# Handing a span's row lists on head by head: where the first expert fetches of a span stand in its search

## The reference, cut to what matters

```python
def peer_block(h, w_peer_q, sub_keys, expert_u, expert_v):
    q = (h @ w_peer_q).reshape(t, PEER_HEADS, 2, PEER_HALF)
    s = jnp.einsum('thcd,chnd->thcn', q, sub_keys, preferred_element_type=jnp.float32)
    s1, i1 = lax.top_k(s[:, :, 0], PEER_TOPK)
    s2, i2 = lax.top_k(s[:, :, 1], PEER_TOPK)
    cand = (s1[..., :, None] + s2[..., None, :]).reshape(...)
    best, sel = lax.top_k(cand, PEER_TOPK)
    eidx = jnp.take_along_axis(cidx, sel, axis=-1)
    g = jax.nn.softmax(best, axis=-1).astype(h.dtype)
    a = jax.nn.gelu(jnp.einsum('thkd,td->thk', expert_u[eidx], h), approximate=False)
    return jnp.einsum('thk,thkd->td', g * a, expert_v[eidx])
```

## Time and profile before

| What | us |
| --- | --- |
| median of 3 runs | 3914.27 |
| the profiled execution, its own time | 3925.3 |
| its span in the profile | 3923.5 |
| VectorE busy | 2617.0 (67%) |
| TensorE busy | 3260.3 (83%) |
| GpSimd busy | 1120.7 (29%) |

### The profile page before, as it was taken

How to read it: one execution, slowest core, us unless ns; L and a number is a source line. 1 busy time by engine, 2 the same in 40 slices (tenths; PEclk the granted TensorE clock), 3 DMA queues, 4 the chain that set the end, 5 groups by cost and what they waited for, 6 DMA issues and landing times.

```text
span 3923.5 us, 36349 instructions
## 1 busy us (share of the span) xinstructions
PE 3260.3 (83%) x10704; PEld 1824.9 (47%) x10704; DVE 2617.0 (67%) x5677; ACT 1405.3 (36%) x4207; POOL 1120.7 (29%) x1252
## 2 busy tenths in 40 slices
PE   6797898488999987777888899877788887787887
PEld 4423787245555443344544454423444444575431
DVE  1364117777757996777687779964777676756874
ACT  1122201485123233666522233333454444222343
POOL 0000001333323333333333334342333333323442
PEclk9897799788999999888899999998888988676899
DMA  2112243699999989999999999998898888999999
GB/s 92 33 36 67 91 150 102 259 399 404 397 364 408 363 316 372 411 407 406 376 426 426 426 414 378 377 389 344 325 368 350 338 360 336 391 401 412 425 421 385
DMA packets 234020, 1289.23 MB, mean 329 GB/s; under 512 B 45468, under 2 KB 59868, under 8 KB 98341
## 3 DMA queue, kind: packets, MB, share of 16 engines
q0 software_dynamic: 152064, 1107.36, 69.5%
q1 hardware_dynamic: 80036, 175.22, 12.6%
q10 hardware_dynamic: 1728, 4.39, 0.3%
HBM read 1273.47 MB, written 13.40 MB: 328 GB/s over the span
## 4 chain that ended last, share of the span: by engine, by line
PE 35%; DMA 27%; DVE 16%; ACT 5%; issue 5%; POOL 1%; SPq 1%; ACTq 0%; DVEq 0%; POOLq 0%
DMA tl_uv<-in_uv,tl_idx 23%; PE tl_y L905 12%; PE tl_f L1151 6%; DVE tl_uv L1490 3%; PE tl_f L1131 3%; PE tl_f L1162 3%; DVE tl_acc L1477 2%; PE tl_f L1177 2%; DMA X<-in_krope 2%; PE tl_f L965 1%; PE tl_f L1075 1%; PE tl_f L1098 1%; DVE tl_eq L1574 1%; POOL tl_uv L837 1%; PE tl_f L1017 1%
## 5 line engine op out<-in xcount | busy, mean ns | idle before, releaser
L1490 DVE CUSTOM_DVE_ANT_0 tl_uv<-tl_uv,tl_h 128x1024 f32<-128x1024 f32 x1056 | 1272.4, 1217 | 706.4 <-DMA tl_uv<-in_uv,tl_idx 680.4
L837 POOL DMA_INDIRECT tl_uv<-in_uv,tl_idx x1056 | 1042.4, 987 | 1941.1 <-PE tl_y L905 1378.7
L905 PE MATMUL tl_y<-tl_uv,tl_diag 128*128 128x512 f32 (+1 forms) x2552 | 1318.6, 659 | 254.9 <-ACT tl_diag L1198 254.8
L905 PEld LDWEIGHTS tl_y<-tl_uv,tl_diag 128*128 128x128 f32 (+1 forms) x2552 | 491.0, 204 | 916.5 <-issue 497.9
L1226 ACT ACTIVATE tl_ge<-tl_a 128x1 f32<-128x1 f32 x1056 | 209.0, 198 | 1248.1 <-DVE tl_a L1490 1246.5
L1477 DVE SCALAR_TENSOR_TENSOR tl_acc<-tl_uv,tl_w,tl_acc 128x1024 f32<-128x1024 f32 x410 | 524.9, 1280 | 67.2 <-ACT tl_w L1210 66.5
L1210 ACT ACTIVATE tl_w<-tl_ge,tl_weight 128x1 f32<-128x1 f32 x1024 | 301.5, 294 | 33.2
L849 POOL TENSOR_TENSOR tl_cand<-tl_tv 128x48 f32<-128x48 f32 (+5 forms) x128 | 66.1, 544 | 784.2 <-DVE tl_ti L1522 626.1
L1151 PE MATMUL tl_f<-H,w_tail 128*128 128x384 f32 (+2 forms) x1024 | 266.0, 417 | 11.6 <-DMA w_tail<-in_w_merge 7.7
L1177 PE MATMUL tl_f<-H,w_tail 128*128 128x384 f32 (+2 forms) x1024 | 265.8, 414 | 10.2 <-DVE H L1717 9.6
L1198 ACT ACTIVATE tl_diag<-K,tl_w 128x128 f32<-128x128 f32 (+1 forms) x638 | 253.6, 397 | 34.4 <-PE tl_y L905 14.1
(11 more groups left out here) (213 smaller groups left out, 3119.4 us busy)
## 6 DMA issues: line engine op xcount, KB each, us to landing
w_tail<-in_w_merge SPq DMA_DIRECT2D x96, 512.0 KB, 7.6
w_tail<-in_w_peer SPq DMA_DIRECT2D x64, 576.0 KB, 7.7
w_tail<-in_w_conv SPq DMA_DIRECT2D x48, 512.0 KB, 7.9
tl_uv<-in_uv,tl_idx POOLq DMA_INDIRECT x1056, 11.4
w_tail<-in_w_mix SPq DMA_DIRECT2D x32, 512.0 KB, 7.6
X<-in_cache SPq DMA_DIRECT2D x64, 128.0 KB
X<-in_x SPq DMA_DIRECT2D x8, 536.0 KB, 6.9
o_y<-tl_acc ACTq DMA_DIRECT2D x8, 512.0 KB, 6.3
```

What stands on the lines that cost most here:

```text
L837: pool.indirect_dma_start(UV[:, u % RING, :], None, d["uv"], bass.IndirectOffsetOnAxis(ap=which, axis=0)).then_inc(landed[u % RING], 16)
L905: mm = pe.matmul(Y[0:m, half * 512:(half + 1) * 512], DG[:, (pe_count[u] - 1) % DIAGS, 0:m], UV[:, u % RING, D + half * 512:D + (half + 1) ...
L1490: dve.tensor_tensor_reduce(UV[:, u % RING, 0:D], UV[:, u % RING, 0:D], HP[:], 1.0, 0.0, ALU.mult, ALU.add, A[:, t % 2, i:i + 1]).then_inc( ...
```

## The change

Heads are put into groups, `HEADS`: in spans 0 to 2 the groups end after head 1, 2, 4 and 8 (of 8), in span 3 there is one. ScalarE's exponential (`powers`) and VectorE's three operations (`shares`) run once for each group, two search steps after the group's last list, and `gset` counts groups. GpSimd no longer waits for `ranked` before a span's first unit but, in the first tile of a span, for the `finish` of the head whose picks it is to fetch. `due` opens the units of a span's own first tile inside its search: `EDGE` says how far the units are at each span's end (56, 296, 696, 1024 in place of 0, 256, 640, 1024), and the units from one edge to the next are spread over the whole of a span (25/25; 23/25 in the last). In span 0's search TensorE does 4 units a step from step 7 on. `by_dve` follows the new places: 450 units are VectorE's, against 418.

```diff
+        HEADS = [[1, 2, 4, PH]] * (NCH - 1) + [[PH]]
+        group = lambda c, h: next(k for k, e in enumerate(HEADS[c]) if h < e)
+        groups_to = lambda c, k: sum(len(x) for x in HEADS[:c]) + k
+        weighed_at = lambda h: 2 * h + 5
+        EDGE = [56, begin[1] + 40, begin[2] + 56, begin[3]]
...
         def due(c, i, lag):
             if c == 0:
-                return 0
-            first, last = begin[c - 1], begin[c]
-            at = passed[c][i + PRE[c]]
-            base = first + (last - first) * 23 * at // (25 * passed[c][-1])
-            return min(base + lag, last, last if lag == LAG_POOL else -(-(base + (base % PICK == 0)) // PICK) * PICK)
+                base = 4 * max(0, i - RANK - 6)
+            else:
+                at = passed[c][i + PRE[c]] * (23 if c == NCH - 1 else 25)
+                base = EDGE[c - 1] + (EDGE[c] - EDGE[c - 1]) * at // (25 * passed[c][-1])
+            open_to = begin[c]
+            if c < NCH - 1:
+                open_to += TOPK * max([e for e in HEADS[c] if i - RANK >= (weighed_at(e - 1) + 2 if e < PH else HC + 4)], default=0)
+            return min(base + lag, open_to, open_to if lag == LAG_POOL else -(-(base + (base % PICK == 0)) // PICK) * PICK)
...
             def issue(u):
-                if u == begin[c]:
+                if t == PARTS[c][0] and t < NP - 1 and i % TOPK == 0:
+                    pool.wait_ge(finished, 2 * (c * PH + i // TOPK + 1))
+                if t == NP - 1 and i == 0:
                     pool.wait_ge(ranked, c + 1)
-                if t == NP - 1 and i == 0:
                     pool.wait_ge(spread, 4)
...
                 for q in range(HC):
+                    if c == 0 and q == 5:
+                        turn(0)
                     units(due(c, RANK + q, 0))
...
-                if c == 0:
-                    turn(0)
...
-                if u == begin[c]:
-                    act.wait_ge(gset, c + 1)
+                if t == PARTS[c][0] and (i == 0 or t < NP - 1 and i % TOPK == 0 and i // TOPK in HEADS[c]):
+                    act.wait_ge(gset, groups_to(c, (group(c, i // TOPK) if t < NP - 1 else 0) + 1))
...
+                def powers(k):
+                    first, past_ = ([0] + HEADS[c])[k:k + 2]
+                    act.wait_ge(paired, (c * PH + past_) * PAIR)
+                    w = GW[:, c % 2, 0:nt, first * TOPK:past_ * TOPK]
+                    act.activation(w, w, ACT.Exp).then_inc(expo, 1)
...
+            def shares(c, k, nt):
+                first, past_ = ([0] + HEADS[c])[k:k + 2]
+                at = groups_to(c, k)
+                sums = SM[:, 0:nt, first:past_]
+                w = GW[:, c % 2, 0:nt, first * TOPK:past_ * TOPK].rearrange("p t (h k) -> p t h k", k=TOPK)
+                dve.wait_ge(expo, at + 1)
+                dve.tensor_reduce(sums, w, AX.X, ALU.add).then_inc(normed, 1)
...
+                if c < NCH - 1:
+                    dve.sem_inc(gset, 1)
...
                 for q in range(HC):
                     units(due(c, RANK + q + 1, LAG_DVE))
                     search(c, q, nt)
+                    for k, e in enumerate(HEADS[c][:-1]):
+                        if q == weighed_at(e - 1):
+                            shares(c, k, nt)
```

More of the change, by code:

```diff
@@ L696, in tail_stage @@
         LAG_ACT, LAG_DVE, LAG_POOL = 3, 6, 8
+        HEADS = [[1, 2, 4, PH]] * (NCH - 1) + [[PH]]
[3 more added lines that the diff above has]
+        EDGE = [56, begin[1] + 40, begin[2] + 56, begin[3]]
         def due(c, i, lag):
             if c == 0:
-                return 0
-            first, last = begin[c - 1], begin[c]
-            at = passed[c][i + PRE[c]]
-            base = first + (last - first) * 23 * at // (25 * passed[c][-1])
-            return min(base + lag, last, last if lag == LAG_POOL else -(-(base + (base % PICK == 0)) // PICK) * PICK)
+                base = 4 * max(0, i - RANK - 6)
[6 more added lines that the diff above has]
+            return min(base + lag, open_to, open_to if lag == LAG_POOL else -(-(base + (base % PICK == 0)) // PICK) * PICK)
         def by_dve(u):
-            c = chunk_of(u // PICK) + 1
-            if c == NCH or u % PICK < 8:
-                return False
-            if due(c, -NCV, 0) <= u < due(c, RANK, 0):
-                return u % 4 != 0
-            return u < due(c, END, 0) and (u % 8 == 7 if u >= due(c, RANK, 0) else u % 2 == 1)
+            if u % PICK < 8:
+                return False
+            for c in range(NCH):
+                if u < due(c, END, 0):
+                    if u >= due(c, RANK, 0):
+                        return u % 8 == 7
+                    return u % 4 != 0 if u >= due(c, -NCV, 0) else u % 2 == 1
+            return False
         pe_count = list(itertools.accumulate(0 if by_dve(u) else 1 for u in range(UNITS)))
@@ L1448, in _ @@
                         indices(q // 2 - 1)
+                    for k, e in enumerate(HEADS[c][:-1]):
+                        if q == weighed_at(e - 1):
+                            powers(k)
                 units(due(c, END + 1, LAG_ACT))
@@ L1451, in _ @@
                 units(due(c, END + 2, LAG_DVE))
-                act.wait_ge(paired, (c + 1) * PH * PAIR)
-                act.activation(GW[:, c % 2, 0:nt], GW[:, c % 2, 0:nt], ACT.Exp).then_inc(expo, 1)
+                powers(len(HEADS[c]) - 1)
                 if c == NCH - 1:
@@ L1565, in pairs @@
                                   IO[:].unsqueeze(1).to_broadcast(full), ALU.is_equal).then_inc(marked, 1)
+            def shares(c, k, nt):
[5 more added lines that the diff above has]
+                dve.tensor_reduce(sums, w, AX.X, ALU.add).then_inc(normed, 1)
+                dve.wait_ge(normed, 3 * at + 1)
+                dve.reciprocal(sums, sums).then_inc(normed, 1)
+                dve.wait_ge(normed, 3 * at + 2)
+                dve.tensor_tensor(w, w, sums.unsqueeze(3).to_broadcast([P, nt, past_ - first, TOPK]), ALU.mult
+                                  ).then_inc(normed, 1)
+                dve.wait_ge(normed, 3 * at + 3)
+                if c < NCH - 1:
+                    dve.sem_inc(gset, 1)
             def finish(c, h, nt):
@@ L1737, in _ @@
                 dve.sem_inc(ranked, 1)
[L1738 to L1746, removed]
+                shares(c, len(HEADS[c]) - 1, nt)
                 if last:
@@ L1751, in _ @@
                     dve.wait_ge(spread, 8)
-                dve.sem_inc(gset, 1)
+                    dve.sem_inc(gset, 1)
             units(UNITS)
```

## The result

The changed kernel takes 3933.47 us (median of 12 runs) against 3913.97 us (12 runs of the kernel before); the ratio is 1.0048, interval 1.0032 to 1.0063. It is slower by 19.5 us. Forecast were 3887 us (27.5 less) and a range of 3838 to 3922; both are wrong, and so is the sign.

A forecast was written before the change was run, and what follows sets the result against it. It took moving expert rows by DMA as the bound from about 719 us on, and a chain over several engines in decode. -152.5 + 96 + 8 - 11 + 12 + 20 = -27.5 us gave 3887 us, range 3838 to 3922.

The forecast's parts named there:

- the places and counts: First fetch near 638 us, span 0's list near 815; fetches by stretch 62 / 244 / 398 / 302 / 50.
- the three starts: Starts of the stages after the searches: loads wait behind further units, 2, 2 and 8 us, together 12 us of cost.
- VectorE is the limit: Span 0's search: a step's 4 fetches take 9.8 us against some 12 of VectorE; the search costs 96 us.
- the term of span 2's search: Span 2's search: 90 units instead of 79, at VectorE's 1.46 us each instead of 2.46: minus 11 us.
- the decode term: Decode stage: 33 fewer units give 61 us, the middle of 40 and 81, so 20 us less than counted.
- the 11 us: Whole kernel: the median of the runs lies 11 us under the profiled execution, turning 3898 into 3887 us.
- one exchange rate: From 719 us on: a fetch taken out of a full stretch is worth 2.46 us; 62 fewer give 152.5 us.
- Rival A: Whole kernel: the DMA queue is the limit everywhere, decode gives all of 81 us; about 3847 us, chance 0.25.
- Rival B: Decode stage keeps its length, 33 units fewer give 0 instead of 61 us; about 3948 us, chance 0.13.
- Rival C: Span 0's search runs at the ring's pace, costing 125 us in place of 96; no change, 3914 us, chance 0.17.
- The delay by VectorE's casts: Span 0's search: by the skill's rule casts would delay fetches; nothing by the median, 1 us a fetch at worst, hidden.

The follow-up runs named there:

- e9: As e5, but TensorE adds all of the first 56 units, 12 of which VectorE added before; 3870.28 us, ratio 0.9882 to the kernel before.
- e1: The changed kernel with one number changed, 697 instead of 696 units at the end of span 2; 3922.14 us, ratio 1.0005 to the kernel before.
- e4: Unit order and VectorE's share of the kernel before, but lists and weights handed on by head groups as in the changed kernel; 3922.27 us, ratio 1.0006.
- e3: The changed kernel without the early start, no unit in span 0's search; 3967.44 us, ratio 1.0122 to the kernel before.
- e2: The changed kernel with own units only in span 0's search, later stages paced as in the kernel before; 3938.32 us, ratio 1.0047.
- e7: As e5, but without early start, units at 0 / 256 / 640 / 1024, no own units in any search; 3934.77 us, ratio 1.0044.
- e8: As e5, but 28 units in span 0's search, 2 a step in place of 4; 3882.4 us, ratio 0.9907 to the kernel before.
- e10: As e5, but 5 units a step in span 0's search and 72 at its end; 3908.2 us, ratio 0.9982 to the kernel before.
- e5: The changed kernel with units at 56 / 300 / 640 / 1024, no own units in span 2's search; 3880.12 us, ratio 0.9906 to the kernel before.
- e6: As e5, but 668 in place of 640 units at span 2's end; 3915.44 us, ratio 0.9993 to the kernel before.

## Why the prediction was wrong

**Right: the places and counts.** The first fetch came at 634 us (638 forecast), the counts at the lists were met, the list of span 0 came at 806 (815). At the three starts TensorE stood 5.7, 16.7 and 25.5 us, where waits of 7 to 20 us were forecast; before it had stood 18.65 us at the third. The forecast called that the wait for the page, but the row names no releaser. The decode span's stretch took 1025 us (1022 forecast, in part by luck, see below) and the rest 146 (145).

**Right in size, only in part in reason: span 0's search.** The stretch cost 88 us instead of 96. "VectorE is the limit" stands only in part: VectorE was busy 152.6 of 172 us, but the DMA share was 0.94, and when e9 took 14 us of work off VectorE, the search got 3 to 5 us shorter.

**Wrong: the term of span 2's search.** The forecast booked 11 more units there as VectorE's 1.46 us each, "minus 11 us" against the rate of the queue, plus three groups. It looked at how many units a search holds and not at how they stand in its steps. The search took 321 us from its first query copy, where the kernel before took 270. 18 us of this is the standstill at the tile's edge, shown by e1; about 6 is the grouping, in e4's profile. The other 27 us (11 more units, 12 in e1: 2.2 to 2.5 us each) are near the rate of the queue after all, where 16 were booked. So this stretch came out at 1165 us instead of 1136. Span 1's search crosses its edge at unit 256 too, with one unit in one of its steps; its stretch took 791 instead of 779. There the trace shows no standstill: around unit 256 GpSimd is never idle for more than 7.4 us before a fetch. Still, that search took 254 us where the kernel before took 234, with 70 fetches against 69; 4 us of it is the grouping (e4 took 238), and the rest stays open. The granted clock of span 2's stretch was lower too, 0.88 against 0.92; e1 and e3, whose places there are the same but for one unit, have 0.89 and 0.88. No run changes the clock alone.

**Wrong: the size of the decode term, hidden by the profiled run.** Forecast were 61 us for 33 fewer units. The trace of the changed kernel from the first page to the first gate has 714 us against 773 before, 58 less, which looks like a hit. By the mark that the forecast named, the first convolution matmul, it is 656 us against 708, where 645 was forecast. But e2, e4, e7, e8 and e9 have the units of the kernel before there, and took 761 to 763 us (e10 769, e5 777). The profiled run of the kernel before, 11 us above its median, was long at just this place; e4, with the same order of units there, took 762. Against the usual length the saving was 47 us (41 in e3). No second profile of the kernel before was taken, so that this is where its 11 us lie is argued, not shown. I had carried the 11 us unchanged through the sum; 10 of them went away with the change of run.

Together: -9 (span 0) + 12 (span 1) + 30 (span 2) + 3 (span 3) is 36 of the 37 us between the forecast and the measured profile (-27.5 and +10), and the long decode stage of the profiled run before would make up the rest up to the medians' +19.5.

**Wrong in kind: one exchange rate.** 2.46 us is what a fetch costs where the queue is full. Measured, the price depends on where it stands: about 1.5 us in span 0's search (88 us / 61), 1.1 to 1.3 in span 1 below some 245 fetches (nothing in e10) and 2.2 above (e2, e3, e8), 2.5 in span 2 on average (e1 less e5: 148 us / 60, unevenly as e6 shows), 1.6 to 1.9 in the decode span (e5 less e1: 93 us / 50; e8 less e1: 78 / 49). The change took 80 fetches from the decode span's price and put 26 into span 2's with a standstill. The forecast did lower the price for decode, but it summed over a move whose worst part it could have priced alone: by its own numbers the 56 own units of span 2 save less than they cost (58 fetches more in span 2 at 2.46 less the 11, and 8 for the start, are 140 us; behind it 33 are worth 61 and 25 at 2.46 another 62). e5 shows this: without them the kernel is 1.4% faster than with them and 0.9% faster than the kernel before. Neither half of the change as made is a gain (e2 1.0047, e3 1.0122); the early start becomes one when its gain is taken out of spans 1 and 2.

Rival A was wrong in the total. Rival B named the right side and the wrong mechanism: the decode stage did get 47 to 58 us shorter, more than the 33 that B allowed. Rival C's place was wrong too, since span 0's search kept to 88 us. The winner was none of them, a standstill and a price in span 2.

The delay by VectorE's casts, one of the prediction's points, did not show in the median of the search that now holds them beside fetches:

```profile
L849 POOL DMA_INDIRECT tl_uv<-in_uv,tl_idx x61: 934/938/1923, 634.0 to 800.7; - x61
```

The median is 938 ns (937 in the earlier trace rows), and the longest 1923. The casts there are of 32 elements a partition. VectorE has one long operation of the kind in that window (L1494, a multiplication by a scalar over 1024 elements, 747 ns from 690.32 us), and the fetch issued beside it at 690.64 us took 1227 ns; e1 and e5 have the same pair, with 1235 and 1230 ns. The Trainium skill (SBUF, "SBUF: two separate sides") holds that GpSimd cannot write a fetch's descriptors while VectorE runs an operation in a two-port mode, such as a copy or cast. The trace agrees at most with 0.3 us in that one place; whether an operation here was in such a mode, no run shows.

## What to carry to other kernels

When work that flows through a ring of buffers is moved from one stage to another, price it in each of the two stages by runs with other counts: a full queue's rate was about the upper end here, and a stage with idle DMA engines gave back as little as half of it. Write down the places step by step for every engine and look for a step with none: a rounding that held an engine at a tile's edge for one step kept GpSimd from fetching for 22 us here, and one unit more cured it. And before one carries a profiled run's distance to its median through a sum, one looks in which stage it lies.

## What the runs showed that I had not expected

The decode stage's length with equal units varies between kernels by 16 us (761 to 777), while some other stages repeat almost exactly: span 0 took 113.3 us from its first gate to the root of its norm in all twelve profiles, and span 1's search 255.9 us in e5 and e6. But the decode stage is not the only place: the root of span 0's norm comes at 601 to 604 us in eleven profiles and at 614 in e4, and span 2's stretch, with the same order of units in it, took 997, 998 and 1007 us in e5, e10 and e9. A difference of 10 us between two profiles means something only in a stage that is known to repeat.
